# A triangular solve in an RWKV-7 layer: from 64x64 chunk matrices to compact 32x32 diagonal blocks

## The chip, the cores and the metric

The kernel runs on one core of one Trainium2 chip. The metric is the device time of one execution in microseconds (us). Times of one execution of the program lie within about 0.3% of each other, so a difference under that can't be told from none.

The engines are named as in the profile: PE is TensorE's matmul, PEld its weight load, DVE is VectorE, ACT is ScalarE, POOL is GpSimd, SP is SyncE, whose queue issues most transfers.

## The reference

Two decoder layers of width 1024 over 256 positions. Each layer mixes tokens with three branches (a gated linear recurrence, differential attention, RWKV-7), merges them with gates, and ends in a gated MLP. Only the RWKV-7 branch is touched. Per head (8 heads of 64), it computes

```python
def step(state, inp):
    r_t, w_t, k_t, v_t, a_t, b_t = inp
    sa = jnp.einsum("bhvk,bhk->bhv", state, a_t)
    state = (state * w_t[:, :, None, :] + sa[..., None] * b_t[:, :, None, :]
             + v_t[..., None] * k_t[:, :, None, :])
    return state, jnp.einsum("bhvk,bhk->bhv", state, r_t)
```

The kernel works in chunks of 64 positions. Within a chunk the recurrence over `sa` is a triangular system: with N the strictly lower triangular 64x64 matrix of the products of the a and b vectors of the chunk's positions (each scaled by its decays), the kernel needs T = (I - N)^-1 for every head and chunk: 8 heads x 4 chunks = 32 inverses a layer.

## The kernel before

Everything of the program is in `trunk_kernel`, with one block of code for each engine; the order of the work on each engine is written out by hand, and semaphores join them. For the merge of the branches TensorE has 576 matmuls a layer (12 token units of "gate" or "merge" weights, 128x128 weights with 512 columns moving; lines 1973, 1975 and 1979) which depend on nothing in the RWKV branch. A generator hands them out: `fill(point)` puts the next `FILL[point]` of them into TensorE's program at a point where it would otherwise wait for another engine, and what is left is issued after the branch.

The 32 matrices of a layer lie as `[128, 2, 8, 64]`: partitions 0 to 63 and 64 to 127 hold the first and the second chunk of a pair, then parity of the head (`par`), then 8 blocks (pair of chunks x head pair). One bank of PSUM holds the 8 blocks of one parity, 512 columns. In this layout the stages of the solve are, in the order of `STEPS`:

- "ak", "n", "nt" (TensorE, `chunk_products`, line 2075): the products of K and A, the matrix N, and N transposed, 32 products of 64x64 each, in four tiles of the array (2 row groups by 2 column groups). DVE reads them out with masks (lines 1499, 1501, 1491).
- The start: T of the 2x2 diagonal blocks is I + N restricted to them. ACT writes identities into T and its transpose TT (lines 874, 875), DVE adds the masked blocks of two (lines 1491, 1515).
- Then TensorE makes the products of AK with V (line 2098), which ACT reads (line 887).
- Five levels (`LEVELS`, block sizes 2, 4, 8, 16, 32), each with two steps for each parity: "m", the product of N and TT, read out by DVE with the level's mask (line 1519), and "x", the product of T with that, added to TT by DVE (line 1525). After every level but the last DVE transposes TT back into T by 32x32 blocks (line 1529); blocks of T beyond 32 aren't needed. A step of TensorE is 16 products of 64x64 (`block_products`, line 2084), on the two diagonal tiles of the array, 32 for both parities; a product in f32 stands in the trace as two weight loads and two matmuls.

After each step TensorE has 8 matmuls of `FILL` (6 after the last one). I call the two parities of a step with the fill behind them a slot; the five levels are ten slots a layer. Beside the reading, DVE takes other work in the solve by place in its program: `mod_beside(1)` (one weight block of the conditioning vectors, lines 1112 and 1115, which waits for a 512 KB transfer that POOL issues, line 560), `gated(2)` (line 1363), `dve_chunks` and `branch_low` (the low parts of weights and inputs, lines 1350 and 1400). POOL makes some low parts itself (line 586). SP's queue reloads the four slots of `ring` with 1 MB of weights each as TensorE finishes them (line 490); the masks are loaded once, in the first layer (lines 524 and 526).

```python
def block_products(b, a, bb, done):
    for m in range(8):
        for c in range(2):
            last = MM(ps[halves[c], b, m * 64:(m + 1) * 64], a[halves[c], m, :], bb[halves[c], m, :], start=True, stop=True)
            if m == 7:
                last.then_inc(done, 1)
```

## Time and profile before

| what | value |
|---|---|
| median of 3 runs | 1099.38 us (1097.0 to 1100.24) |
| the profiled execution | 1098.47 us, its span 1096.7 us |
| mean granted clock of TensorE | 0.992 of full |
| busy: PE, PEld, DVE, ACT, POOL | 1075.3, 989.9, 845.3, 582.7, 125.8 us |
| solve of layer 0 (first product to the last read-out) | from 209.5 to 261.1 us of the span |
| solve of layer 1 | from 745.2 to 793.3 us |

A row of the timeline gives start, duration, engine, line, operation, tile written and read, shape and count, and in brackets how long the engine was idle before it and what released it. "issue" as the releaser means that the engine waited for nothing that the profile shows.

### The profile page before, as it was taken

Reading aid. Unit: us, or ns where it says so; the run is one execution under the profiler, and the core shown is the slowest. Engines: PE = TensorE matmul, PEld = TensorE weight load, DVE = VectorE, ACT = ScalarE, POOL = GpSimd, SP = SyncE. Lnnn points to the kernel's source line nnn. Section 1 sums busy time; section 2 is a strip of 40 time slices with the busy share of each in tenths; the row PEclk is TensorE's granted clock in tenths of the full one; section 3 lists DMA queues with packets and bytes.
Section 4 is the critical chain, followed back from the end, with each engine's and each line's share of the span. In section 5 each row is a group of like instructions: output and inputs, shape, how many; then the busy total and the mean of one; then the engine's idle time right before and its main releaser. Section 6 shows DMA issues by size and latency. Waiting matters only on the chain.

```text
span 1096.7 us, 23323 instructions
## 1 busy us (share of the span) xinstructions
PE 1075.3 (98%) x9660; PEld 989.9 (90%) x9660; DVE 845.3 (77%) x1245; ACT 582.7 (53%) x894; POOL 125.8 (11%) x142
## 2 busy tenths in 40 slices
PE   8999999899999999999999999999999999999997
PEld 7889988787789999999989999878887999999997
DVE  4798998686578798987758899977755878888763
ACT  2266567532364666663355575683227466666533
POOL 0100000056002000001120000002640200000001
PEclk8999999999999999999999999999999999999999
DMA  9946455443156567667854546361615465555651
GB/s 378 342 172 217 178 172 225 180 154 139 42 208 235 188 233 245 218 234 292 311 189 167 206 157 223 144 229 60 232 59 192 154 244 184 186 191 191 222 201 39
DMA packets 41460, 214.81 MB, mean 196 GB/s; under 512 B 7936, under 2 KB 8320, under 8 KB 22048
## 3 DMA queue, kind: packets, MB, share of 16 engines
q1 hardware_dynamic: 29856, 171.65, 42.8%
q0 software_dynamic: 11520, 41.95, 10.8%
q8 instruction: 64, 1.05, 0.4%
q14 instruction: 20, 0.16, 0.0%
HBM read 212.01 MB, written 1.05 MB: 194 GB/s over the span
## 4 chain that ended last, share of the span: by engine, by line
PE 93%; DVE 4%; DMA 2%; issue 1%; ACT 1%; DVEq 0%; ACTq 0%
PE ps L1786 18%; PE ps L1784 17%; PE ps L1785 17%; PE ps L1975 6%; PE ps L1979 6%; PE ps L1973 6%; PE ps L1804 5%; PE ps L2084 2%; DMA mring<-wmod_dram 2%; PE ps L1743 1%; DVE macc L1115 1%; PE ps L2256 1%; PE ps L2075 1%; PE ps L1761 1%; PE ps L2000 1%
## 5 line engine op out<-in xcount | busy, mean ns | idle before, releaser
L965 ACT ACTIVATE WH<-ring 128x1024 fp32r<-128x1024 f32 x144 | 151.9, 1060 | 164.9 <-PE ps L1786 157.2
L1634 DVE TENSOR_TENSOR WLO<-ring,WH 128x1024 fp32r<-128x1024 f32 x144 | 175.8, 1234 | 70.0 <-ACT WH L965 70.0
L1786 PE MATMUL ps<-HH,WLO 128*128 128x256 f32 x736 | 208.1, 283 | 0.0
L1785 PE MATMUL ps<-HL,WH 128*128 128x256 f32 x736 | 206.6, 281 | 0.0
L1784 PE MATMUL ps<-HH,WH 128*128 128x256 f32 x736 | 205.0, 279 | 0.0
L1786 PEld LDWEIGHTS ps<-HH,WLO 128*128 128x128 f32 x736 | 138.7, 188 | 0.0
L1784 PEld LDWEIGHTS ps<-HH,WH 128*128 128x128 f32 x736 | 138.5, 188 | 0.0
L1785 PEld LDWEIGHTS ps<-HL,WH 128*128 128x128 f32 x736 | 138.0, 188 | 0.0
L560 POOL DMA_DIRECT2D mring<-wmod_dram x80 | 43.4, 542 | 763.2 <-DVE macc L1115 456.5
L1115 DVE SCALAR_TENSOR_TENSOR macc<-mring,sm,macc 128x1024 f32<-128x1024 f32 x70 | 96.5, 1378 | 16.4 <-DMA mring<-wmod_dram 14.4
L1786 PE MATMUL ps<-GH,WLO 128*128 128x256 f32 x384 | 108.3, 282 | 0.0
L1784 PE MATMUL ps<-GH,WH 128*128 128x256 f32 x384 | 108.2, 282 | 0.0
L1785 PE MATMUL ps<-GL,WH 128*128 128x256 f32 x384 | 107.9, 281 | 0.0
L1786 PE MATMUL ps<-HG,RLO 128*128 128x256 f32 x384 | 107.9, 281 | 0.0
L1662 DVE SCALAR_TENSOR_TENSOR TK<-ps,PR,TK 128x255 f32<-128x255 f32 x192 | 79.1, 475 | 0.0
L1979 PE MATMUL ps<-RLO,HG 128*128 128x512 f32 x192 | 77.7, 405 | 0.0
L1786 PEld LDWEIGHTS ps<-GH,WLO 128*128 128x128 f32 x384 | 73.7, 192 | 0.0
L1786 PEld LDWEIGHTS ps<-HG,RLO 128*128 128x128 f32 x384 | 72.5, 189 | 0.0
L1785 PEld LDWEIGHTS ps<-GL,WH 128*128 128x128 f32 x384 | 72.2, 188 | 0.0
L1784 PEld LDWEIGHTS ps<-GH,WH 128*128 128x128 f32 x384 | 72.1, 188 | 0.0
L778 ACT ACTIVATE WC<-ring 128x1024 fp32r<-128x1024 f32 x36 | 37.8, 1055 | 62.3 <-PE ps L1975 33.1
L1784 PE MATMUL ps<-HG,WCR 128*128 128x256 f32 x208 | 58.8, 283 | 0.0
(404 smaller groups left out, 2552.7 us busy)
## 6 DMA issues: line engine op xcount, KB each, us to landing
ring<-wmain_dram SPq DMA_DIRECT2D x150, 1024.0 KB, 4.9
mring<-wmod_dram POOLq DMA_DIRECT2D x80, 512.0 KB, 5.0
G<-wmod_dram SPq DMA_DIRECT2D x3, 1024.0 KB, 10.0
R<-wmod_dram SPq DMA_DIRECT2D x3, 1024.0 KB, 17.7
TK<-wmod_dram SPq DMA_DIRECT2D x2, 1024.0 KB, 20.5
X<-x_t_dram SPq DMA_DIRECT2D x1, 1024.0 KB, 5.8
y_dram<-H SPq DMA_DIRECT2D x4, 256.0 KB, 2.1
SW<-small_dram SPq DMA_DIRECT2D x1, 512.0 KB, 13.6
```

Source lines behind the costliest of these rows:

```text
L560: pool.dma_start(mring[:, n % 2, :], wmod[mod_row(n)]).then_inc(s_m[n % 2], 16)
L965: A(WH[:, n % 2, part], ring[:, b, part], ACT.Copy).then_inc(hi_ready, 1)
L1115: V.scalar_tensor_tensor(macc[:, u % 2, :], block, sm[:, CSIL + kt:CSIL + kt + 1], macc[:, u % 2, :], ALU.mult, ALU.add).then_inc(mod_used, 1)
L1634: V.tensor_tensor(WLO[:, n % 2, part], ring[:, b, part], WH[:, n % 2, part].bitcast(F32), ALU.subtract).then_inc(lo_ready, 1)
L1662: ins = V.scalar_tensor_tensor(UB[:, q % 2, t, d:S], duo(b)[:, t, 0:S - d], PR[:, l, bass.ds(j + (COL["fw"] + 48 * (2 - d)), 1)], UB[:, q ...
L1784: MM(out, w_high[:, at], high, start=start, stop=False, skip_group_check=True)
L1785: MM(out, w_high[:, at], low, start=False, stop=False, skip_group_check=True)
L1786: return MM(out, w_low[:, at], high, start=False, stop=stop, skip_group_check=True)
L1804: last = MM(ps[:, g % 4, m * S:(m + 1) * S], w_of(g, m, i), rhs[:, i, :], start=(i == 0), stop=(i == KT - 1))
L1973: MM(ps[:, b, :], high[:, tk], w_high, start=(k == 0), stop=False, skip_group_check=True)
L1975: i = MM(ps[:, b, :], low[:, tk], w_high, start=False, stop=False, skip_group_check=True)
L1979: i = MM(ps[:, b, :], high[:, tk], w_low, start=False, stop=(k == nk - 1), skip_group_check=True)
```

## The change

The matrices of the levels up to 16 become compact: only the two diagonal 32x32 blocks of each 64x64 matrix are kept, one on each quarter of 32 partitions, so that the matrices of one parity are `[128, 8, 32]`, and the four 32x32 tiles on the diagonal of the array work on them. Masks come in this shape too (`CN`, eight more DMAs in the first layer; `CM` keeps three masks).

- "n" is 64 products with 32x32 results (64 rows of weights, 32 columns; eight tiles); "nt" is gone, and "off" is new: 32 products for the block N[32:64, 0:32], which ACT copies to `No` (two copies of 128x256).
- The start: T = I + N masked, formed compactly (`Tn`), and its transpose `TTn` by DVE's 32x32 transposes in place of a product; ACT's two identities are gone.
- A step of a level below the last is 32 products of 32x32 per parity (64 for both) in place of 16 of 64x64; DVE reads 128x256 in place of 128x512.
- The last level is T22 N21 T11 alone: its "m" is 16 products per parity, its "x" 32, of which half multiply with an identity to bring the second diagonal block into place; DVE copies. Before it, one DVE operation ("left") writes the first diagonal block and zeros into the 64x64 `TTm`.
- `mod_beside(1)` of the "x" of the fourth level moves to the "m" of the last; the number is the same. `FILL` stays as it is.

```diff
-LEVELS = [M_U2, M_U4, M_U8, M_U16, M_U32]
+LEVELS = [N_U2, N_U4, N_U8, N_U16, None]
+LAST = len(LEVELS) - 1
...
+        Nn, No, Tn, TTn, Mn = [narrow_mats(a) for a in (4, 6, 8, 10, 12)]
...
+                    for g in range(4):
+                        rows = slice(Q * g, Q * g + Q)
+                        sp.dma_start(CN[rows, N_LOW:N_ID, :], consts[rows, AT_MASKS:AT_MASKS + N_ID * P]
+                                     .rearrange("p (n s) -> p n s", s=P)[:, :, Q * g:Q * g + Q]).then_inc(s_masks, 16)
+                        sp.dma_start(CN[rows, N_ID, :], consts[rows, Q * g:Q * g + Q]).then_inc(s_masks, 16)
...
-                A(TTm.rearrange("p g m s -> p (g m) s"), over(small_mask(M_ID), 16), ACT.Copy).then_inc(i_ready, 1)
-                A(Tm.rearrange("p g m s -> p (g m) s"), over(small_mask(M_ID), 16), ACT.Copy).then_inc(i_ready, 1)
...
+                for par in range(2):
+                    act.wait_ge(t_mm, SOLVED[-1] * l + products_until("off", par))
+                    A(No[:, par], narrow(4 + par), ACT.Copy).then_inc(off_ready, 1)
...
                     elif kind == "n":
-                        V.tensor_tensor(Nm[:, par], oct(b), over(small_mask(M_LOW), 8), ALU.mult).then_inc(t_ev, 1)
+                        V.tensor_tensor(Tn[:, par], narrow(b), over(narrow_mask(N_L1), 8), ALU.mult).then_inc(t_ev, 1)
+                        V.tensor_tensor(Nn[:, par], narrow(b), over(narrow_mask(N_LOW), 8), ALU.mult).then_inc(t_ev, 1)
                         if par:
                             for p2 in range(2):
+                                dve.wait_ge(t_ev, base + reads_until("begin", p2))
+                                V.tensor_tensor(Tn[:, p2], Tn[:, p2], over(narrow_mask(N_ID), 8), ALU.add).then_inc(step, tick(n_step))
                             for p2 in range(2):
+                                dve.wait_ge(step, n_step[0] - 1 + p2)
+                                V.transpose(flat(TTn[:, p2]), flat(Tn[:, p2])).then_inc(t_init, 1)
                             dve_chunks(18, 19)
...
+                    elif v < LAST:
+                        V.tensor_tensor(TTn[:, par], TTn[:, par], narrow(b), ALU.add).then_inc(t_ev, 1)
+                        if par == 1:
+                            for p2 in range(2):
+                                dve.wait_ge(t_ev, base + reads_until("x", p2, v))
+                                V.transpose(flat(Tn[:, p2]), flat(TTn[:, p2])).then_inc(t_turned, 1)
+                            if v == LAST - 1:
+                                V.tensor_scalar(TTm[:, :, :, 0:Q].rearrange("p g m s -> p (g m) s"), TTn.rearrange("p g m s -> p (g m) s"),
+                                                small_mask(M_U32)[:, CH - 1:CH], None, ALU.mult).then_inc(t_ev, 1)
+                                gated(2)
+                            else:
+                                mod_beside(1)
                     else:
-                        V.tensor_tensor(TTm[:, par], TTm[:, par], oct(b), ALU.add).then_inc(t_ev, 1)
...
+                        V.tensor_copy(TTm[:, par, :, Q:CH], narrow(b)).then_inc(t_ev, 1)
...
-                def block_products(b, a, bb, done):
+                def block_products(b, pairs_, done):
 
                     for m in range(8):
-                        for c in range(2):
-                            last = MM(ps[halves[c], b, m * 64:(m + 1) * 64], a[halves[c], m, :], bb[halves[c], m, :], start=True, stop=True)
+                        for g, a, bb in pairs_:
+                            last = MM(ps[quarters[g], b, m * Q:(m + 1) * Q], a[:, m, :], bb if len(bb.shape) == 2 else bb[:, m, :],
+                                      start=True, stop=True)
                             if m == 7:
                                 last.then_inc(done, 1)
...
-                chunk_products(6, KK, AB, t_mm)
-                pe.wait_ge(t_ev, base + 2)
-                chunk_products(4, AB, KK, t_mm)
+                narrow_products(6, [(g, g, g) for g in range(4)], t_mm)
+                pe.wait_ge(t_ev, base + reads_until("ak", 1))
+                narrow_products(4, [(1, 1, 0), (3, 3, 2)], t_mm)
```

## Rows read from the trace of the kernel before

**Rows 1.** The page: busy time by engine, and the queue that brings TensorE's code.

```profile
PE 1075.3 (98%) x9660; PEld 989.9 (90%) x9660; DVE 845.3 (77%) x1245; ACT 582.7 (53%) x894; POOL 125.8 (11%) x142
...
q8 instruction: 64, 1.05, 0.4%
```

**Rows 2.** Timeline of layer 1: the first two slots of the solve.

```profile
753.09 1.94 PEld L2084 LDWEIGHTS ps<-R 64*64 64x64 f32 x64 [0.36 <-issue]
...
754.86 1.28 DVE L1519 TENSOR_TENSOR R<-ps,CM 128x512 f32<-128x512 f32 x2
...
757.16 1.95 PEld L2084 LDWEIGHTS ps<-R 64*64 64x64 f32 x64 [0.36 <-issue]
...
759.92 1.30 DVE L1529 STREAM_TRANSPOSE R<-R 128x512 f32<-128x512 f32 x2
```

**Rows 3.** Windows of layer 0: slots, the opening, and two stretches with a gap.

```profile
core 0: us, PE busy (x) PEld busy (x) DVE busy (x) ACT busy (x) POOL busy (x), PEclk, DMA share, GB/s
...
209.50:212.30 2.80, 2.27 (x139) 2.13 (x140) 2.58 (x4) 0.00 (x0) 0.00 (x0) 1.00 0.60 237
212.30:214.60 2.30, 0.24 (x11) 0.11 (x5) 0.94 (x2) 0.00 (x0) 0.00 (x0) 0.98 0.08 29
214.60:218.00 3.40, 3.39 (x91) 3.39 (x92) 1.60 (x5) 0.00 (x0) 0.00 (x0) 0.51 0.02 5
221.00:225.10 4.10, 4.10 (x75) 3.40 (x74) 3.55 (x4) 2.59 (x4) 2.48 (x1) 1.00 0.02 4
...
237.30:241.40 4.10, 4.10 (x75) 3.41 (x74) 3.79 (x4) 4.00 (x8) 1.54 (x3) 1.00 0.81 299
...
258.30:261.90 3.60, 3.60 (x71) 2.98 (x71) 1.91 (x3) 0.00 (x0) 2.57 (x2) 1.00 0.43 146
265.50:271.00 5.50, 5.50 (x170) 4.38 (x168) 3.35 (x6) 1.29 (x3) 5.34 (x5) 1.00 0.52 194
```

**Rows 4.** Timeline of layer 1: 128-wide transposes, then 64x64 products in four and two tiles.

```profile
737.33 0.94 PEld L2062 LDWEIGHTS ps<-C,KK 128*128 128x128 f32 x8
...
745.22 1.02 PEld L2075 LDWEIGHTS ps<-KK,ZS 64*64 64x64 f32 x64 [0.35 <-issue]
...
749.04 1.94 PEld L2098 LDWEIGHTS ps<-TK,R 64*64 64x64 f32 x64 [0.17 <-DVE R L1501]
```

**Rows 5.** Timeline of layer 0: the two gaps of TensorE that no semaphore explains.

```profile
214.61 1.65 PE L2075 MATMUL ps<-KK,AB 64*64 64x64 f32 x51 [2.07 <-issue]
...
272.58 0.80 PE L2149 MATMUL ps<-R,TK 64*64 64x64 f32 x35 [1.40 <-issue]
```

**Rows 6.** DMA in windows 215.7:216.9, then 270.1:271.2 and 220:226 (40 slices each).

```profile
q8 instruction: 1, 0.02, 6.0%
...
DMA  0009000000000000000000000000000000000000
...
DMA  0000000400000000000000000000000000000000
```

**Rows 7.** Lines of the solve on DVE and ACT: one operation in ns (min, median, max).

```profile
L1491 DVE TENSOR_TENSOR E<-ps,CM x4: 415/420/425, 216.4 to 749.4; 128x256 f32<-128x256 f32 x4
...
L1529 DVE STREAM_TRANSPOSE R<-R x16: 662/685/706, 227.8 to 786.8; 128x512 f32<-128x512 f32 x16
...
L874 ACT ACTIVATE R<-CM x2: 1042/1043/1044, 198.2 to 734.0; 128x1024 f32<-128x1024 f32 x2
```

**Rows 8.** Timeline of layer 0: ACT before its reading, and one of DVE's conditioning blocks.

```profile
218.10 0.60 ACT L887 ACTIVATE WY<-ps 128x512 f32<-128x512 f32 x1 [8.82 <-PE ps L2098]
...
247.21 1.28 DVE L1115 SCALAR_TENSOR_TENSOR macc<-mring,sm,macc 128x1024 f32<-128x1024 f32 x1 [1.80 <-DMA mring<-wmod_dram]
```

**Rows 9.** Timeline of SP's queue: the masks and the next weights.

```profile
34.62 4.26 SPq L524 DMA_DIRECT2D CM<-consts_dram  x1
...
41.84 3.37 SPq L526 DMA_DIRECT2D CM<-consts_dram  x1
46.90 67.29 SPq L490 DMA_DIRECT2D ring<-wmain_dram  x12
```

More of the change, by code:

```diff
@@ L185, with tiles_used, solve_reads, products_until @@
 STEPS = solve_steps()
-NSTEP = len(STEPS)
-SOLVED = [int(n) for n in np.cumsum([1 if k in ("ak", "n", "nt") else 2 for k, _, _, _ in STEPS])]
-def step_no(kind, par, v):
-    return next(i for i, s in enumerate(STEPS) if s[:3] == (kind, par, v))
+def tiles_used(kind, v):
+    return {"ak": 1, "n": 4, "off": 2, "m": 2 if v == LAST else 4, "x": 4}[kind]
+SOLVED = [int(n) for n in np.cumsum([tiles_used(k, v) for k, _, v, _ in STEPS])]
+def solve_reads():
+    reads = []
+    for kind, par, v, _ in STEPS:
+        if kind == "n":
+            reads += [("begin", par, 0), ("n", par, 0)]
+        elif kind != "off":
+            reads.append((kind, par, v))
+        if (kind, par, v) == ("x", 1, LAST - 1):
+            reads.append(("left", 0, 0))
+    return reads
+READS = solve_reads()
+NREAD = len(READS)
+def products_until(kind, par, v=0):
+    return SOLVED[next(i for i, s in enumerate(STEPS) if s[:3] == (kind, par, v))]
+def reads_until(kind, par, v=0):
+    return READS.index((kind, par, v)) + 1
 def trunk_kernel(nc, wmain, wmod, small, v1v2, params, consts, lqk, x_t, positions, y_t):
@@ L370, in oct, with narrow @@
             return ps[:, b, :].rearrange("p (m s) -> p m s", s=CH)
+        def narrow(b):
+            return ps[:, b, 0:8 * Q].rearrange("p (m s) -> p m s", s=Q)
         def by_chunk(ap, c):
@@ L1487, in _ @@
                 dve_chunks(17, 18)
-                def blocks_of_two(at, src, mask, odd):
-                    m = over(every_other(small_mask(mask), odd), 8)
-                    return V.tensor_tensor(E[:, at, :].rearrange("p (j n) -> p j n", j=8), every_other(src, odd), m, ALU.mult)
-                dve.wait_ge(s_masks, 64)
-                base = NSTEP * l
+                dve.wait_ge(s_masks, 192)
+                base = NREAD * l
                 mm0 = SOLVED[-1] * l
                 for n, (kind, par, v, b) in enumerate(STEPS):
+                    if kind == "off":
+                        continue
                     dve.wait_ge(t_mm, mm0 + SOLVED[n])
@@ L2064, in _ @@
                 fill(7)
-                base = NSTEP * l
+                base = NREAD * l
                 halves = [slice(64 * i, 64 * i + 64) for i in range(2)]
+                quarters = [slice(Q * i, Q * i + Q) for i in range(4)]
                 def chunk_products(b0, a, bb, done):
```

83 lines of the change are left out of this document (43 added, 40 removed).

## The prediction, made before the changed kernel was run

> **What bounds the kernel now.** I read the page first: PE is busy for 98% of the span [rows 1], so what counts in any stretch is TensorE's own stream, unless the change makes it wait. Then the timeline of the solve. A slot of layer 1 starts at 753.09 and the next at 757.16, a period of 4.07 us [rows 2]: 64 pairs of weight load and matmul (32 products, two pairs each) and 8 matmuls of the fill behind them. DVE reads out and transposes beside this, two operations in 1.28 and 1.30 us [rows 2], and isn't what the slot ends on: in the windows of 221.0 and 237.3 PE is busy throughout [rows 3]. ACT idles 8.82 us before its reading [rows 8]. So the solve is bound by TensorE.
>
> Then the rate of TensorE. In two tiles 64 pairs begin within 1.94 us [rows 2]; less one load's 0.135 this is 28.7 ns a pair, or 57 ns a pair on each tile. In four tiles 64 pairs take 1.02 us [rows 4], 14 ns a pair, again 56 ns on each tile. So the tile sets the pace and not the issue, at least down to 14 ns. Eight 128-wide pairs take 0.94 us [rows 4], 107 ns each: width costs about 0.8 ns a column, with some 5 ns beside it.
>
> Last the gaps that no semaphore explains. In layer 0 TensorE stops twice in the middle of a run of small products, until 214.61 and until 272.58, and the profile says "issue" [rows 5]. The queue named instruction brought 64 packets and 1.05 MB [rows 1], 16 KB each. One of them begins in the fourth of 40 slices of the window from 270.1, at 270.2, and takes some 0.97 us; PE resumes 1.4 us after it has landed [rows 5, 6]. Counting instructions back from the gap at 212.3, 279 began since 209.5 [rows 3]; counting back from the second, the 338 of the window from 265.5 [rows 3] put the 256th before the stop at about 267.0. I read this as: a packet is 256 instructions (128 pairs), two packets fit, and the next is asked for when the last begins to run. From that moment until the new one runs it was 209.7 to 214.6, 4.9 us, and 267.0 to 272.6, 5.6 us. The transfers were busy then (0.60 and 0.52 of the DMA engines [rows 3]). With nothing else to carry, the packet of the window from 220 begins at 221.1 [rows 6], at once, and would have run 1.0 + 1.4 = 2.4 us after the request; the one in the window from 215.7 had been asked for at 214.6, so 3.7 us. Now a slot spends 72 pairs in 4.07 us, 128 pairs in 7.2, and this costs nothing. It is the part of the machine that the change leans on.
>
> **What the change does to TensorE, part by part.** A layer's "n" and "nt" are 128 pairs now, at 14 ns: 1.8 us. The ten steps are 640 pairs at 28.7 ns: 18.4 us. After, "n" and "off" are 192 pairs, the steps 8 x 128 + 64 + 128 = 1216 pairs, 32 columns wide. No row shows such a pair. By the tile's pace of 0.8 ns a column and 5 ns it takes 30 ns on its tile, in four tiles 7.6 ns. If each pair still took 14 ns, the least seen, the steps would come to 17.0 us and the slot would stay as it is. I take 7.6, because two tiles and four gave the same pace per tile, and keep 14. The slot would then be 4.07 - 1.84 + 0.97 = 3.2 us. Unbound by anything else this gives 18.4 - 9.2 = 9.2 us a layer in the steps and 0.4 us in the opening, 19 us in all.
>
> The Trainium skill ("TensorE: Matmul & The Clock Gate", section "Wait — 56ns, not 53.3ns?") says that the start of a matmul never follows that of the last within about 25 ns, however narrow. By that the slot would be 4.07 - 1.84 + 3.2 = 5.4 us, and the change a loss of some 25 us. The trace doesn't agree: its 64 pairs in 1.02 us are 14 ns apart.
>
> But the code has to come. After, a slot is 136 pairs and some waits, 1.07 packets. Four slots lie where the DMA engines are nearly idle (0.02 at 221.0), six where they are busy (0.81 at 237.3, 0.43 at 258.3) [rows 3].
> - The four quiet slots: 4.3 packets, each the larger of 3.0 us (its run time at 3.2 us a slot) and 2.4 to 3.7 us for the fetch, say 3.15: 13.5 us for 16.3 now. -2.8 us.
> - The six busy ones, of which one has 64 pairs less: 5.9 packets at 2.4 to 5.6 us, of which those under 3.0 count as 3.0; I take 4.2, a bit over the middle, since the busy transfers are packed closer. 24.8 us, where now it is 237.3 to 261.9, 24.6 us [rows 3]. +0.2 us.
> - The opening has 320 pairs in place of 256, and less time in them. In layer 0 the packet awaited at 212.3 still comes at 214.6. What follows in it, 128 pairs, is through in 1.3 us where it took until 221.0 less the fill, and the next packet runs at 214.6 + 3.7 = 218.3. The rest of AK by V at 30 ns (1.6 us) and the fill (some 2.4 us) end at 222.3, for 221.0 now. +1.2 us, in layer 1 taken the same.
>
> The sum is -1.4 us a layer. Beside it the clock: after the 2.3 us gap of layer 0 its granted share was 0.51 from 214.6 to 218.0 [rows 3], a loss of 1.7 us. Layer 1 has no such gap now and gets one; at even chances +0.9 us, 0 to 1.7. And DVE's conditioning blocks: one already waited 1.80 us for its transfer [rows 8], and it is asked for relatively later; +0.4 us (0 to 3). In all -2.8 + 1.3 = -1.5 us on the executed 1098.47, which lies 0.9 us under the median.
>
> **What costs nothing, and what hides it.** DVE reads 256 columns at 0.42 us for 0.68, and transposes in about the same ratio from 0.685 [rows 7]: 28 operations a layer save about 7 us, which keeps pace with TensorE's shorter slot; without it DVE would have bound, since it is busy 3.5 to 4.0 of each 4.1 us now [rows 3]. The new operation "left" (0.4 to 0.7 us) stands in the slot that loses a conditioning block of 1.3 us. ACT loses two copies of 1.04 us [rows 7] outside the path and gets two of 0.4 us before its reading of AK by V, inside an idle time of 8.82 us [rows 8]; without that cover, 0.8 us. SP issues 12 mask transfers for 4: those took from 34.6 to 45.2, and the next weights followed at 46.9 [rows 9], so 1.7 us are free, and I guess 2 to 6 us more. The weights land 5 us after the issue and aren't used before 59; if that cover were gone, it would cost up to 4 us once. POOL's queue is passed by nothing.
>
> **The rivals.**
> (1) The code keeps up (0.24). The fetch was seen to bind twice, both times with busy transfers, and could start earlier when the request is not behind a wait. Then the 3.2 us slot holds: -9.2 - 0.4 a layer, given back 2 us a layer to conditioning blocks that come late: about -15 us, 1084 us. The Trainium skill ("Runtime: NRT & Kernel Launch", section "Instruction fetch mechanics") has it so: crossing a block of 256 instructions is mostly hidden. The two gaps speak against this as a rule.
> (2) The issue floor lies near 14 ns (0.12). Then TensorE saves nothing in the slots, the packets come nearly in time, and the result is 0 to +4 us: 1101 us.
> (3) The other side (0.14): gaps beget a slow clock. The place is the busy half of the solve, where a packet may come 2.5 us late; the price is the 1.7 us that the stretch from 214.6 shows. If such a gap comes in three of the six slots of each layer, this is +5 a layer, with the gaps' own time in the sum above at 5.6 us a packet (5.9 x 5.6 = 33.0, +8.4 a layer) about +23 us, 1122 at the most, 1110 in the middle. It decides once the gaps reach about 2 us. For it: DMA at 0.81 and more for whole slots. Against: the slots have 1.9 us of full-width fill each, and the second gap of layer 0 left the clock alone.
> That the change doesn't compute in 32x32 tiles side by side (each product waiting for the last one: 30 ns a pair) I count within (3): two tiles do overlap within one bank [rows 2].
>
> **The numbers.** The forecast has 0.50. Less than 0.3% (3.3 us) can't be told from no change here. Its own range is 8 us less to 6 us more: of its 0.50, 0.14 are faster, 0.27 the same, 0.09 slower. (1) adds 0.22 faster and 0.02 same; (2) 0.07 same and 0.05 slower; (3) 0.14 slower. So faster 0.36, same 0.36, slower 0.28. Time: 1098.47 + 0.9 - 1.5 = 1097.9, say 1098. The likeliest case's own range is 1091 to 1105. The range for 8 in 10 reaches into (1) and (3): 1087 to 1110.
>
> **What would show it.** In the changed trace: runs of 128 pairs in about 1.0 us where they aren't interrupted (7.6 ns a pair), or 1.8 (rival 2). Slots of 3.2 to 3.5 us in the quiet stretch and of 4 to 5 in the busy one, with PE's idle time put down to "issue", and packets of the instruction queue 3 to 5 us apart, each 1.4 us ahead of the resumption. Ten more packets on the page, 74 for 64 (1280 more instructions a layer are five). A gap near 747.3 in layer 1. I am wrong if the slots are 3.2 us throughout, if PE waits for DVE and not for "issue", or if the granted clock falls under 0.98.

## The result and the profile after

The changed kernel took 1119.85 us (median of 4 runs, 1113.06 to 1124.19), the kernel before beside it 1098.19 us: a ratio of 1.019, 95% interval 1.0142 to 1.0239. It is slower by some 21 us (1.9%), where 1098 us were forecast and 1110 us closed the range. The four runs of the changed kernel lie 1.0% apart, more than the 0.3% given ahead for one program; the intervals take that in. The profiled execution is the fastest of the four: 1113.06 us, span 1111.2 us, mean granted clock 0.982 (0.992 before).

The page of the changed kernel, sections 1, 3 and 4:

```profile
PE 1072.7 (97%) x10940; PEld 983.6 (89%) x10940; DVE 827.5 (74%) x1243; ACT 580.2 (52%) x894; POOL 125.1 (11%) x142
...
q8 instruction: 74, 1.21, 0.4%
...
PE 93%; DVE 3%; issue 3%; ACT 1%; POOL 1%; DMA 0%; DVEq 0%; ACTq 0%
```

The busy time of PE hardly fell (1075.3 us before), although half of the time of the levels' products was to go, 18 of 37 us over both layers; the queue named instruction has its 74 packets, for 64 [rows 1]; and "issue" has 3% of the chain, 33 us, where the page of the kernel before has 1%. What PE waited for, by line and releaser:

```profile
PE ps L2135 <- issue: 14.4, 8, 4.0
...
PE ps L2126 <- issue: 3.7, 2, 2.1
PE ps L2017 <- issue: 1.3, 1, 1.3
```

Each row gives the total in us, how often, and the longest. L2135 is the products of the levels, L2126 those of "n" and "off". The kernel before had the two gaps of [rows 5]. The view has no row in which L2135 waits for DVE. In the timeline of PE, one undisturbed slot, a gap in a quiet stretch, and the worst one:

```profile
224.87 1.56 PE L2135 MATMUL ps<-R 32*32 32x32 f32 x128
226.36 0.50 PE L2011 MATMUL ps<-WCG,HG 128*128 128x512 f32 x1
...
764.56 0.49 PE L2013 MATMUL ps<-WCG,HGL 128*128 128x512 f32 x1 [0.20 <-issue]
764.98 1.37 PE L2135 MATMUL ps<-R 32*32 32x32 f32 x127
768.57 0.21 PE L2135 MATMUL ps<-R 32*32 32x32 f32 x1 [2.21 <-issue]
...
775.39 1.65 PE L2135 MATMUL ps<-R 32*32 32x32 f32 x128
...
779.00 1.14 PE L2135 MATMUL ps<-R 32*32 32x32 f32 x99
784.12 0.64 PE L2135 MATMUL ps<-R 32*32 32x32 f32 x29 [3.99 <-issue]
```

The fill starts 1.49 us after the first of 128 pairs (226.36 for 224.87). In the slot of the kernel before, 64 pairs start at 753.10 in the timeline of PE and the first matmul of the fill at 755.11, 2.01 us later. The starts of 128 pairs that nothing disturbs span 1.20 us, 9.4 ns a pair, for 1.86, and such slots follow each other in 3.37 us (221.50 to 224.87), for 4.07: some 0.7 us shorter. But then a slot stops in its middle for 3.99 us. The transfers while it waits:

```profile
q1 hardware_dynamic: 42, 0.34, 67.6%
q0 software_dynamic: 39, 0.15, 32.2%
q8 instruction: 1, 0.02, 4.9%
```

This is the window from 781.5 to 782.7. Queues 1 and 0 (the weight ring and the conditioning blocks) fill the DMA engines, and the one packet of code among them lands at 782.62, 1.5 us before PE resumes. All the larger gaps look so: 1.4 to 1.6 us lie between a landing and the resumption at 246.04 and 247.44, 767.0 and 768.57, 802.85 and 804.39. Counting back 256 instructions from each resumption, as the prediction did, gives the request: from request to run it is 3.4 to 4.0 us for packets in the quiet stretches (222.1 to 225.55, 232.6 to 236.17, 764.56 to 768.57), and 5.2, 6.1 and about 7.6 us for those that ran at 241.31, 247.44 and 784.12.

The gap that ends at 768.57 has the DMA engines almost to itself (nothing but the packet of code from 765.5 until 767.0), and still lasts 2.21 us. What sets it apart is what its packet holds: the one that began at 764.56 is one matmul of the fill and 127 narrow pairs, some 1.8 us of work against 4.0 us until the next one runs. A packet with eight matmuls of the fill in it lasts 3.2 us and hides most of the fetch. So it is the work of each packet that counts, and not the mean of a slot.

The ten slots of layer 0 in the kernel before, from the first product to the end of the last, with columns as in [rows 3]:

```profile
221.00:260.40 39.40, 38.80 (x714) 32.34 (x713) 33.60 (x38) 11.22 (x15) 22.73 (x15) 1.00 0.47 172
```

Those of the changed kernel, layer 0 and layer 1, then some of its stretches at half the clock:

```profile
221.50:262.00 40.50, 34.76 (x1292) 27.61 (x1292) 28.65 (x40) 10.55 (x14) 22.04 (x15) 0.96 0.46 163
757.80:805.00 47.20, 36.94 (x1290) 28.82 (x1290) 24.09 (x40) 11.26 (x15) 22.90 (x15) 0.88 0.42 148
...
565.10:568.50 3.40, 3.40 (x10) 2.69 (x9) 3.30 (x6) 3.37 (x8) 0.57 (x1) 0.50 0.00 0
...
769.90:773.30 3.40, 3.40 (x133) 2.52 (x131) 0.95 (x2) 0.00 (x0) 2.55 (x2) 0.50 0.34 99
783.60:790.40 6.80, 6.28 (x166) 4.92 (x165) 2.69 (x5) 1.06 (x1) 3.77 (x3) 0.50 0.42 144
804.00:807.40 3.40, 3.01 (x10) 1.84 (x9) 0.42 (x1) 0.00 (x0) 0.00 (x0) 0.50 0.02 5
...
sum 34.00, PE 31.73 PEld 26.16 DVE 16.44 ACT 9.82 POOL 9.82; mean PE 3.97 PEld 3.27 DVE 2.05 ACT 1.23 POOL 1.23
```

Layer 0 is no shorter than before and layer 1 is 7 to 8 us longer. Leaving out the start and the end of the program, TensorE has 34.0 us at 1.2 GHz in eight stretches, where the kernel before has two of 3.4 us. Five of the eight, 23.8 us, come with the five gaps of 2 us and more: that at 783.6 begins 0.5 us before its gap of 3.99 us ends, that at 804.0 0.4 us before the end of one of 3.31 us, that at 769.9 1.3 us behind one of 2.21 us. The other three (565.1, 739.2 and 896.2) have no gap over 0.45 us near them, and lie outside the solves. If time at half the clock costs half of itself, which is an estimate (the fill ran at half its pace there, the narrow pairs at 13.4 ns for 9.4), 27.2 us more of it is 13.6 us: 10.2 with the gaps, 3.4 without.

The balance of the two profiled executions: by the spacing of their pairs, the products of the slots give back 2 x 6.8 us = 13.6 us. Idle time of PE in gaps over 0.45 us rose from 6.7 to 22.6 us, +15.9, and the clock took 13.6. That makes +15.9; the spans differ by 14.5, since some idle time falls into the stretches at half clock and so is counted twice. By place: +1.0 us up to the state chain of layer 0 (its start of the solve was 1.5 us earlier, the solve 2.5 us longer), +2.3 between the solves, +9.9 in the solve of layer 1 (63.3 us to the reading products, for 53.4) and +1.2 behind it. The 3.5 us between and behind the solves, where nothing was changed, are about the size of the falls of the clock there, so they need not be an effect of the change.

### The profile page after: what moved, and what is told of

Its sections match the earlier page's. It is cut to its first block, busy times and chain, and to the rows that moved or that the text cites. A ratio compares the mean times of both kernels' runs of the same rounds, so it can differ in the third digit from the quotient of the medians.

```text
span 1111.2 us, 25891 instructions
## 1 busy us (share of the span) xinstructions
PE 1072.7 (97%) x10940; PEld 983.6 (89%) x10940; DVE 827.5 (74%) x1243; ACT 580.2 (52%) x894; POOL 125.1 (11%) x142
## 4 chain that ended last, share of the span: by engine, by line
PE 93%; DVE 3%; issue 3%; ACT 1%; POOL 1%; DMA 0%; DVEq 0%; ACTq 0%
PE ps L1824 17%; PE ps L1822 17%; PE ps L1823 17%; PE ps L2013 6%; PE ps L2017 6%; PE ps L2011 6%; PE ps L1842 5%; PE ps L2135 3%; PE ps L1781 1%; PE ps L2314 1%; PE ps L1799 1%; PE ps L2038 1%; PE ps L1968 1%; DVE RLO L1623 1%; PE ps L2100 1%
## 5 line engine op out<-in xcount | busy, mean ns | idle before, releaser
L1154 DVE SCALAR_TENSOR_TENSOR macc<-mring,sm,macc 128x1024 f32<-128x1024 f32 x70 | 92.1, 1316 | 15.7 <-DMA mring<-wmod_dram 13.2
L817 ACT ACTIVATE WC<-ring 128x1024 fp32r<-128x1024 f32 x36 | 37.8, 1055 | 69.8 <-PE ps L2013 43.9
L1842 PE MATMUL ps<-H,ring 128*128 128x256 f32 x256 | 60.2, 397 | 0.9 <-DVE H L1186 0.5
## 6 DMA issues: line engine op xcount, KB each, us to landing
SW<-small_dram SPq DMA_DIRECT2D x1, 512.0 KB, 14.4
```

What stands on the lines that cost most here:

```text
L1154: V.scalar_tensor_tensor(macc[:, u % 2, :], block, sm[:, CSIL + kt:CSIL + kt + 1], macc[:, u % 2, :], ALU.mult, ALU.add).then_inc(mod_used, 1)
L1842: last = MM(ps[:, g % 4, m * S:(m + 1) * S], w_of(g, m, i), rhs[:, i, :], start=(i == 0), stop=(i == KT - 1))
```

## The experiments

Ratios are to the kernel before, run beside it on the same chip, with 95% intervals; a time without an interval is one run, read for its trace and not for its time. "The after" is the changed kernel.

### Is it the code? Fewer products, more fill, pairs by themselves

**More fill between the products.** Edit of the after: 10 matmuls of fill instead of 8 (6 at the last) at each of eleven points, and `gated(2)` moved a slot forward with them.

```diff
-FILL = [8, 32, 48, 32, 36, 8, 20, 8] + [8] + [8, 8] * 4 + [8, 6]
+FILL = [8, 32, 48, 32, 36, 8, 20, 8] + [10] + [10, 10] * 4 + [10, 10]
```

> The changed kernel with 10 matmuls of the fill behind each step of the solve in place of 8 (11 points, the total of the kernel unchanged), and one DVE read of a merge bank a slot earlier so that they can run. Theory A (the code of TensorE comes too slowly: a packet of 128 weight-load and matmul pairs needs 3.4 us at least and up to 6 us under load): a packet then lasts 0.4 us longer per slot, so the stalls called issue shrink by 5 to 8 us over both layers and one to three of the slow-clock stretches go; the time falls by 4 to 12 us against the changed kernel's 1120 us. Rival B (32-wide products are slow in themselves, by issue or by tile): the work is only moved, the time stays within 2 us.

1142.96 us, 1.0409 (1.0367 to 1.0451): a miss. The gaps in the products stayed (14.0 us put down to "issue" at L2135, for 14.4), although a slot had two matmuls more. They still end 1.3 to 1.6 us behind a landing, but this run doesn't bear out that a little more work in each packet shortens them; why it doesn't stays open. And the fill, pulled forward, came to its weights' low parts too soon (6.8 us of waiting for L1389). It shows what a pause can cost, though. The windows before and after such a wait:

```profile
285.00:289.70 4.70, 3.03 (x80) 2.77 (x80) 2.34 (x4) 0.00 (x0) 4.70 (x5) 1.00 0.00 0
289.70:323.80 34.10, 33.43 (x169) 26.24 (x170) 8.91 (x11) 1.99 (x5) 2.34 (x2) 0.50 0.20 77
```

A wait of 2.34 us (288.03 to 290.37), and the clock stayed at half for 34.1 us, though PE was busy through 33.4 of them. The record of the clock is no artefact: matmuls of the fill began every 0.43 us there, for 0.23 at the full clock.

**Twice the pairs at half the width**, to price a pair. Edit of the before: each 64x64 product in two of 32 moving columns.

```diff
-    last = MM(ps[halves[c], b, m * 64:(m + 1) * 64], a[halves[c], m, :], bb[halves[c], m, :], start=True, stop=True)
+    for s in (0, 32):
+        last = MM(ps[halves[c], b, m * 64 + s:m * 64 + s + 32], a[halves[c], m, :], bb[halves[c], m, s:s + 32], start=True, stop=True)
```

> The kernel before, with each 64x64 product of the ten steps issued as two products of 32 moving columns: the same result, 128 pairs in each slot as in the changed kernel, but no other part of the change. Theory A: undisturbed a slot's products take 2.4 us or less in place of 1.86, the slot 4.6 us or less, a packet 4.3 us, so the quiet slots gain no stall and the busy ones do: 5 to 15 us slower than before, with resumptions 1.4 us after a code packet has landed, and 5 more packets a layer. Rival B: slower by the products' own time alone, 10 x 0.5 us a layer, 10 us, with no stall that no semaphore explains. The two are told apart by the gaps, not by the total.

1133.87 us, 1.0332 (1.0291 to 1.0374), 37 us more where 5 to 15 were expected. The pairs of a slot:

```profile
224.21 3.94 PE L2085 MATMUL ps<-R 64*64 64x32 f32 x128
```

Their starts span 3.72 us, 29.3 ns a pair in two tiles: what a pair with 64 moving columns takes. So the 57 ns that I had read as the price of 64 moving columns is the price of the 64x64 weights. The period of a slot became 5.93 us and no product of the slots waited for code, with as many pairs in a slot as the after has: the time per packet matters, not the count.

**The pairs alone**, at the end of the before: 512 products with 32x32 weights in the four diagonal tiles, then 512 with 64x64 weights and 32 columns.

```diff
+            for n in range(512):
+                g = n % 4
+                q4 = slice(32 * g, 32 * g + 32)
+                MM(ps[q4, 5, n // 4 % 16 * 32:n // 4 % 16 * 32 + 32], ones[q4, 0:32], ones[q4, 0:32], start=True, stop=True)
...
```

> The kernel before with a run of 512 products of 32x32x32 in the four diagonal tiles at TensorE's end (1024 pairs, 8 packets of code, nothing else to transfer), then 512 products of 64x64 weights by 32 moving columns in two tiles (1024 pairs). Theory A: bursts of 128 pairs in 1.2 us (9.4 ns a pair), then a wait until 1.4 us after the next packet has landed, a period of about 3.4 us for 128 pairs, 27 us for each of the two runs. Rival B: an even rate without gaps, 9.4 ns a pair or whatever the tile allows: 10 us for the first run. The second run also gives the pace of a 64x64 weight load with 32 columns: by the tile 18 ns a pair.

1171.1 us. The timeline of PE:

```profile
1088.93 1.28 PE L2324 MATMUL ps<-ones 32*32 32x32 f32 x128 [2.19 <-issue]
1093.23 1.93 PE L2324 MATMUL ps<-ones 32*32 32x32 f32 x128 [3.02 <-issue]
1096.70 1.93 PE L2324 MATMUL ps<-ones 32*32 32x32 f32 x128 [1.54 <-issue]
1100.72 1.93 PE L2324 MATMUL ps<-ones 32*32 32x32 f32 x128 [2.09 <-issue]
...
1104.46 1.93 PE L2324 MATMUL ps<-ones 32*32 32x32 f32 x128 [1.81 <-issue]
```

and two windows of it:

```profile
1100.00:1114.00 14.00, 7.84 (x494) 7.37 (x495) 0.00 (x0) 0.00 (x0) 0.00 (x0) 0.50 0.02 5
1120.00:1140.00 20.00, 20.00 (x380) 20.00 (x380) 0.00 (x0) 0.00 (x0) 0.00 (x0) 0.50 0.01 2
```

This is the clearest row of the study. Bursts are of exactly 128 pairs, 256 instructions. The second follows the first in 4.30 us, with the output's transfer beside it; from there on they follow each other every 3.47 to 4.02 us, 3.75 at the end, with no other transfer (DMA share 0.02). So code comes at 128 pairs in about 3.75 us when it is asked for like this, and PE ran them in 1.09 (8.5 ns a pair, in the one burst shown at full clock). And the clock was at half: from 1090.5, in the first pauses, through the second set of products, in which PE was busy all the time. There a pair with 64x64 weights took 53 ns, for 29.3 at the full clock.

The Trainium skill has this otherwise ("Runtime: NRT & Kernel Launch", section "Instruction fetch mechanics"): the next block of 256 instructions is fetched while one executes, and the crossing is "mostly hidden". That holds here as long as a packet's work takes longer than the 3.4 to 4.0 us of a quiet fetch, as in the slots of the before; it fails for narrow products.

**Half of the products left out** of the ten slots of the after (blocks 4 to 7 of the inverses are not computed in its levels, and DVE adds half as much in the "x" steps).

```diff
-                    for m in range(8):
+                    for m in range(4):
                         for g, a, bb in pairs_:
...
```

> The changed kernel without half of the products of the ten steps (the second four of the eight blocks; their inverses stay at the start's value, and DVE adds half as much in the x steps): 64 pairs in a slot again, 32 wide. Theory A (packets of code of 128 pairs, at least 3.4 us apart): a slot is 0.6 + 0.37 + 1.86 = 2.85 us, a packet 5 us; the gaps called issue in the slots vanish but for one or two of the busiest, and with them the slow-clock stretches there; ten slots in 29 to 32 us in both layers (changed kernel: 40 and 47). Rival B (narrow products are slow to switch or to issue): half of the gaps stay and ten slots take 34 us or more.

1107.53 us. Quiet slots came to 2.82 us and every code gap in the slots was gone, but the ten slots still took 37.8 and 37.5 us, a miss. PE's waits name the next bound (L2136 is the products of the levels here, L2127 those of the opening):

```profile
PE ps L2136 <- DVE R L1558: 11.3, 6, 4.6
PE ps L2127 <- issue: 4.9, 2, 2.9
```

### What lies under the code: VectorE's conditioning blocks

**The blocks moved away**, all eight of a layer behind the state chain (their transfers too), in the after.

```diff
                         elif par == 1:
-                            mod_beside(1)
...
+                mod_beside(8)
                 dve.wait_ge(gg_ready, 4 * (l + 1))
```

> The changed kernel with the seven conditioning blocks of each layer's solve (their transfers by POOL and their DVE work) put behind the state chain; the total will be longer, since they are then waited for, and is not what is looked at. Theory A: with fewer transfers beside it a code packet is carried sooner; in the solve no slot loses more than 2.5 us, and the ten slots of a layer take 33 to 38 us in place of 40 (layer 0) and 47 (layer 1). Rival C (DVE's conditioning blocks, waiting for their transfers, hold the steps): also shorter, but the gaps called issue stay as they were. If the slots stay at 40 and 47 with the same gaps, the lag of the packets has another source.

1148.38 us. The slots took 38.9 us in layer 0 and 42.2 in layer 1, a miss (33 to 38 were expected), and kept 10.9 us of code gaps, with 5.9 us more in the opening; and TensorE waited 29.8 us behind the state chain, where the moved blocks stand before low parts of weights. Against the kernel before (39.4 us), taking away either bound alone gains 2 us a layer at the most and loses 3 in one; against the changed kernel it does help in layer 1 (47.2 us). Taking away both:

> The changed kernel with half of the products of its ten steps left out (64 instructions of a slot's 128 pairs, its numbers wrong for it) and, also, its eight conditioning blocks of the solve and state chain moved behind the state chain: both suspected bounds off at once. Theory (two bounds lie stacked, code delivery and VectorE's blocks, each of which alone keeps the ten slots at 37 to 40 us): here the slots follow TensorE's own work, about 2.8 to 3.0 us each, so ten slots take 28 to 31 us from the first slot's start to the end of the last, and the idle of TensorE within them is under 2 us a layer. Rival (a third bound: VectorE's reads, masks and transposes of the steps themselves, or ScalarE and the loads of fill weights): ten slots stay over 34 us though no conditioning block and no code gap stands in them. The whole time tells little, since the moved blocks are waited for later (29.8 us in the run that moved them alone): 1105 to 1145 us.

1115.4 us with the same two edits together (the same products left out). The ten slots as windows:

```profile
222.80:249.00 26.20, 26.20 (x682) 20.14 (x682) 15.98 (x32) 10.66 (x15) 18.23 (x8) 1.00 0.33 123
763.00:791.30 28.30, 26.44 (x682) 20.20 (x682) 14.55 (x32) 11.25 (x15) 18.77 (x8) 1.00 0.32 114
```

The slots ran at 2.81 us in both layers, 26.2 and 28.3 us for ten (one code gap of 1.85 us in layer 1), where each edit alone left 38 to 42. Two bounds lie one on the other about the slot of the before, at 3.7 to 4.2 us on average.

**Fast products with half the code**: the before, with both parities of a step together in the four 64x64 tiles, the odd parity crossing from one half of the partitions to the other and back.

```diff
+    for m in range(8):
+        for par in range(2):
+            for c in range(2):
+                fr, to = (c, c) if par == 0 else (c, 1 - c) if kind == "m" else (1 - c, c)
+                last = MM(ps[halves[to], b + par, m * 64:(m + 1) * 64], a[halves[fr], par, m, :], bb[halves[fr], par, m, :], ...)
```

> The kernel before with both parities of a step issued together in all four 64x64 tiles: the odd parity's m product is written to the other half of the partitions, T of that parity is kept there (DVE's transposes in two halves), and its x product comes back. The number of products and of instructions is that of before, 64 pairs a slot, in 1.0 us in place of 1.86 by the pace of four tiles. Theory A: 72 pairs in 3.2 us or more are a packet in 5.7 us, which code delivery allows outside the busiest transfers; DVE has 7.0 us of work in two slots and becomes the bound: 3.5 us a slot, 5 to 14 us faster than before. Rival B (any shortening of the products is lost): within 3 us of before.

1107.0 us, 1.012 (1.0063 to 1.0178), a miss. A slot's products take 0.94 us and quiet slots 3.15 to 3.25, with no code gap among them. DVE is what is late now:

```profile
PE ps L2093 <- DVE R L1530: 11.7, 6, 4.2
PE ps L2093 <- DVE R L1524: 11.2, 7, 2.6
```

and its own timeline, with POOL's beside it, tells why:

```profile
230.81 2.38 POOL L586 TENSOR_TENSOR RLO<-ring,WC 128x1024 fp32r<-128x1024 f32 x1
...
231.03 3.25 DVE L1115 SCALAR_TENSOR_TENSOR macc<-mring,sm,macc 128x1024 f32<-128x1024 f32 x1
234.20 1.27 DVE L1530 TENSOR_TENSOR R<-R,ps 128x512 f32<-128x512 f32 x2
...
243.25 1.28 DVE L1115 SCALAR_TENSOR_TENSOR macc<-mring,sm,macc 128x1024 f32<-128x1024 f32 x1 [3.70 <-DMA mring<-wmod_dram]
```

A block takes 1.28 us alone and 3.25 here beside POOL's operation, and it may wait 3.70 us for its transfer, with the read-out of the products queued behind it. Both were there before ([rows 8] shows a wait of 1.80 us), inside a slot that was long enough. The Trainium skill ("SBUF — State Buffer", section "Who interferes with whom") calls the port pair that VectorE and GpSimd share an exclusive lock; the rows agree, 3.25 us being about the block's 1.28 behind most of POOL's 2.38.

With the blocks moved behind the state chain, as above:

> The kernel before with both parities of a step in four 64x64 array tiles (slot products 0.94 us instead of 1.86) and the eight conditioning blocks of a layer moved behind the state chain. Theory (the four-tile version lost because VectorE, behind its conditioning blocks and their transfers, could not follow a shorter slot): the waits of the slots for VectorE's reads, 23 us in the run with the blocks in place, fall under 5 us, quiet and busy slots alike take 3.1 to 3.3 us, ten slots of a layer 31 to 33 us. The blocks are then waited for later, so the whole time is not lower for it: 1105 to 1150 us. Rival (the four-tile form itself slows VectorE, by its partition-crossing transposes and longer dependence from product to product): the waits for VectorE's reads stay over 12 us.

1111.03 us, 1.0116 (1.008 to 1.0153). The waits of the slots for DVE fell from 22.9 to 2.0 us and ten slots took 30.9 us; the waits came back as 27.8 us behind the state chain, as expected.

### The parts of the change that help, and where the blocks belong

**Only the first twin by vector transposes**, in the before: "nt" is left out, and DVE transposes T once it is formed.

```diff
-    steps = [("ak", 0, 0, 4), ("ak", 1, 0, 5), ("n", 0, 0, 6), ("n", 1, 0, 7), ("nt", 0, 0, 4), ("nt", 1, 0, 5)]
+    steps = [("ak", 0, 0, 4), ("ak", 1, 0, 5), ("n", 0, 0, 6), ("n", 1, 0, 7)]
...
+                            for p2 in range(2):
+                                dve.wait_ge(step, n_step[0] - 1 + p2)
+                                V.transpose(flat(TTm[:, p2]), flat(Tm[:, p2])).then_inc(t_init, 1)
```

> The kernel before with one part of the change alone: the product for N transposed is gone, T of the start is formed as before and its twin by DVE's 32x32 transposes. TensorE loses 64 pairs and one wait for DVE a layer (0.9 + 0.7 us) and half a packet of code, DVE keeps its 2.8 us. Theory A: 2 to 5 us faster than before, no new gap. If it is slower, DVE's start is on the path.

1094.9 us, 0.9979 (0.9965 to 0.9994): this part of the change gains some 2.3 us (0.7 to 3.8). Together with the four 64x64 tiles:

> The two edits of e6 and e7 together. Theory A: their gains add, 7 to 17 us faster than before, 1080 to 1090 us. If code delivery takes it back: less than the better of the two alone, with gaps called issue in the busy slots.

1104.52 us, 1.0077 (1.0057 to 1.0097), a miss: the two gains don't add, and PE waits 21.8 us for DVE's reads. And the twin with the last level on its one off-diagonal block, in the wide layout:

> The kernel before with the first transposed twin by vector transposes (the version that ran at 0.998 of before) and, also, the last level on its one off-diagonal 32x32 block, in the wide layout: the same number of instructions, but with 32x32 weights, 16 pairs to a parity in two array tiles. Theory (in this form the slots are bound by the loading of 64-column weights, some 29 ns a pair, and the code comes in time): the two slots of the last level have products of about 0.5 to 1.0 us instead of 1.86, which saves 0.9 to 1.4 us in each, 2 to 5 us in all with two layers; some comes back as a wait for VectorE, which then has to copy two blocks of 32 partitions. Total 1091 to 1096 us, ratio to before 0.993 to 0.998. Rival (all that a shorter slot gives up is taken by code or VectorE at once, as in the changed kernel): 1096 to 1100 us.

1096.4 us, 0.9977 (0.9957 to 0.9997): no more that can be told than the twin alone. A slot of the last level in it:

```profile
249.18 1.29 PE L2095 MATMUL ps<-R 32*32 32x32 f32 x64
250.40 0.51 PE L1981 MATMUL ps<-RLO,YH 128*128 128x512 f32 x1
```

The fill starts 1.22 us after the first product, for 2.01, and PE waits 1.42 us for DVE's read-out in each layer instead. The starts of the 64 pairs span 1.10 us, 17.4 ns a pair in two tiles, or 35 ns on a tile with 32x32 weights, where 64x64 weights with the same 32 moving columns took 58.6. Whether the rows or the columns of the weights make the difference isn't separated.

**The blocks where VectorE waits.** Edit of the version with twin and four 64x64 tiles: of eight blocks a layer three stay in the slots, one stands before the state chain and four in it, where DVE waited 1.2 to 3.8 us for TensorE with all eight moved away. Their transfers move too, so that POOL's chunks no longer stand behind a wait for DVE.

```diff
-                    if i < 7:
-                        mod_blocks(m1 + i, m1 + i + 1)
+                    if i in (2, 4, 6):
+                        mod_blocks(m1 + i // 2 - 1, m1 + i // 2)
...
+                mod_blocks(m1 + 3, m1 + 4)
...
                                 gated(2)
-                            mod_beside(1)
...
                 gated(3)
+                mod_beside(1)
...
-                        if c == 1:
-                            mod_beside(1)
+                        mod_beside(1)
+                mod_beside(1)
```

> The kernel before with the first transposed twin by vector transposes and both parities of a step in four 64x64 array tiles (together 1.0077 of before), and now the eight conditioning blocks of a layer spread over the places where VectorE waits: one in each of three slots, one behind the reads before the state chain, four in the state chain, where the trace of the version with all eight moved shows VectorE waiting 1.2 to 3.8 us for TensorE at each step; GpSimd's transfers of the blocks move with them, so its chunk work no longer waits for VectorE. Theory (the four-tile slots lost only because the blocks stood in them, and the blocks cost nothing where VectorE waits): the ten slots of a layer take 31.5 to 34 us instead of 40, TensorE waits less than 3 us a layer for VectorE's reads and less than 3 us for low parts of weights, and each layer is 4 to 9 us shorter than in the kernel before. Total 1080 to 1092 us, ratio to before 0.983 to 0.995. Rival (the time that the solve gives up is taken back behind it, by fill work that has been used up or by transfers that come late, as a wait of TensorE between the state chain and the next stage): 1094 to 1108 us.

1077.35 us, 0.9822 (0.9783 to 0.9862). It beats both kernels, by 20 and by 42 us. The windows of its ten slots, PE's waits on them, and DVE in the state chain:

```profile
216.00:247.30 31.30, 29.72 (x713) 23.12 (x713) 28.33 (x39) 11.00 (x15) 21.90 (x11) 1.00 0.43 154
738.40:769.70 31.30, 29.70 (x713) 23.07 (x713) 28.32 (x39) 11.04 (x15) 21.87 (x11) 1.00 0.40 149
```

```profile
PE ps L2092 <- DVE R L1523: 2.9, 6, 0.8
```

```profile
268.27 1.22 DVE L1350 TENSOR_TENSOR RLO<-ring,WC 128x1024 fp32r<-128x1024 f32 x1
269.41 1.28 DVE L1115 SCALAR_TENSOR_TENSOR macc<-mring,sm,macc 128x1024 f32<-128x1024 f32 x1
```

Ten slots take 31.3 us in each layer, the clock is at 1.00, DVE is busy for 28.3 of them, and the block at 269.41 fills what was a wait of 1.29 us in the run with all eight moved. The last two runs separate the placement from the form of the products. The same placement in the after:

> The changed kernel with its eight conditioning blocks a layer spread as in the version at 0.982 of before (three in the slots, one before the state chain, four in it). Theory (code delivery is a bound of its own, 128 pairs in no less than 3.4 us and up to 6 us under ring loads, and falls of the clock follow its gaps): TensorE still idles 6 to 14 us over both solves in gaps that end 1.3 to 1.5 us after a packet has landed, ten slots of a layer take 35 to 38.5 us, and the kernel comes to 1088 to 1112 us: better than the changed kernel (1120), but 10 us or more behind the version in four 64x64 tiles (1077) whose slots need half the code. Rival (the blocks' transfers were what held the packets up, and the blocks what held the slots): slots of 3.1 to 3.4 us throughout, 1070 to 1085 us.

1112.23 us, 1.0148 (1.0101 to 1.0194): 35 us behind. PE's waits, the gap in a slot of layer 0, and the ten slots of each layer:

```profile
PE ps L2135 <- issue: 12.3, 8, 3.0
PE ps L2126 <- issue: 5.8, 2, 4.3
```

```profile
243.29 0.38 PE L2135 MATMUL ps<-R 32*32 32x32 f32 x21
246.71 1.70 PE L2135 MATMUL ps<-R 32*32 32x32 f32 x107 [3.04 <-issue]
```

```profile
224.00:262.80 38.80, 33.73 (x1167) 26.26 (x1169) 19.83 (x34) 11.48 (x15) 19.66 (x10) 0.91 0.36 125
759.50:796.00 36.50, 31.22 (x1161) 24.59 (x1160) 19.13 (x34) 11.06 (x15) 19.29 (x10) 1.00 0.38 132
```

DVE is idle for half of these slots (busy 19.8 us of 38.8), and the code still comes late. And the same placement in the kernel before, its products as they were:

> The kernel before, with nothing changed but where its eight conditioning blocks of a layer stand (three in the slots, one before the state chain, four in it). Theory (its slots of 4.1 us are bound by TensorE's own work and hide the blocks; a block hinders only a shorter slot): the slots stay at 4.07 to 4.1 us, only those above that (the last three of a layer) lose their excess, 0 to 2 us a layer; total 1092 to 1098 us, ratio 0.995 to 1.001. Rival (the placement itself is most of the gain of the version at 0.982): 1080 to 1088 us.

1096.24 us, 0.9988 (0.9966 to 1.001): nothing. So neither the placement nor a faster product gains by itself, and the two together with the twin gain 20 us, 18 more than the twin alone, as long as the code of a slot stays at 64 pairs.

## Why the prediction was wrong

- **The mechanism was named, and it is the one that decides; the steps that failed are the prices of a packet of code and of the clock.** Runs of 128 pairs, packets of 256 instructions, waits put down to "issue" that end about 1.4 us after a landing, 74 packets, a gap near 747.3 (at 751.7): all there. With DVE's conditioning blocks spread, the changed kernel still has 18.1 us of waits for "issue", as many as without, and with half of the products left out it has none in its slots.
- **"2.4 to 3.7 us for the fetch, say 3.15" failed.** I took 2.4 from a packet whose transfer began "at once" with the request that I counted. Code was not short there. In the kernel before the same count has two more begin within 0.2 us of the request (226.81, 234.54) and one 1.1 us ahead of it (248.51), so where code isn't short the count doesn't give the moment of the request. In the changed trace none of those traced back began sooner than 0.9 us after it, and a quiet one takes 3.4 to 4.0 us from request to run; in the run of the pairs alone the packets come 3.47 to 4.02 us apart. So the quiet slots, too, are bound by code: four of them took 14.2 us in layer 0 and 17.6 in layer 1 (757.78 to 775.39), for 13.5. The 17.6 have a second cause, the mean over a slot: the packet of 764.56, with almost no fill in it, left a gap of 2.21 us.
- **"7.6 ns a pair" failed by a quarter.** It is 9.4 in the kernel, 8.5 alone. The working took a tile's pace to go by the width of the product; the split products show that the moving columns don't set it, the size of the weights does. Worth 1.8 x 127 ns = 0.23 us a slot, some 4 us in all; the undisturbed slot is 3.37 us, for 3.2. The Trainium skill's floor of 25 ns from start to start ("TensorE: Matmul & The Clock Gate", section "Wait — 56ns, not 53.3ns?") is further off still: the traces have 8.5 and 9.4 ns.
- **"2.4 to 5.6 us, I take 4.2" for a busy packet was too low.** The three traced back above took 5.2, 6.1 and 7.6 us, two of them outside the bounds, whose upper end came from two packets only. Ten slots up to the next stage's first product were forecast at 13.5 + 24.8 = 38.3 us, for 40.9 before, and took 41.4 in layer 0 (221.50 to 262.93) and 49.6 in layer 1 (757.78 to 807.38), half clock included. The opening took 2.0 us more than before in layer 0 and 1.3 in layer 1, for 1.2 forecast.
- **"+0.9 us for the clock" is the largest miss: 13.6 us in the profiled execution, 10.2 of it with gaps.** I priced one fall, of 1.7 us, in the opening of layer 1. Five stretches came with gaps, for one in the kernel before, and three without, for one. The prediction's rival (3) had this mechanism, with 0.14, 1110 us as its middle and 1122 at the most. Its condition (a gap of about 2 us in three of the six busy slots of each layer) was met in size but not in place: 2.12 and 2.60 us in layer 0, the first of them in the opening, and 2.21, 3.99 and 3.31 in layer 1, the first in the quiet slots. What I set against it, that the second gap of layer 0 left the clock alone, was one gap of 1.4 us and told nothing of those over 2 us. Over the traces of all the kernels here but the one with the pairs alone, start and end left out, 37 of the 43 gaps of 2 us or more come with a stretch at half the clock that begins in them or within 2 us behind them, and 3 of the 53 between 1 and 2 us; 21 stretches of 3.4 us come without any such gap. With about 2 us of a gap seen to cost 1.7 us more in the kernel before, the losing side had deserved more than its 0.28.
- **The wait for DVE's blocks (+0.4) did not come**: the code came later still. It was the second bound, hidden behind the first, as the 11.3 us of the run with half of the products show.
- The gain of the first twin, which the sum had not set apart, is real, 2.3 us.

How much of the +21 us is idle time and how much is the clock can't be read to the microsecond: runs of the after lie between 1113 and 1124 us, and only the fastest has a trace. The clock has most of the spread, though: its mean was 0.982 and 0.981 in the runs of 1113 and 1116 us and 0.973 and 0.975 in those of 1124, which by the estimate above is 7 to 10 of the 8 to 11 us. What makes the clock fall at one gap and not at another stays open as well, as does how the requests queue behind the other transfers: those of the busy packets began 2.8 to 5.0 us after their request, for 0.9 to 1.6 in the quiet.

## What to carry to other kernels

Small products have a price in code: before cutting matmuls into more and narrower ones, divide the instructions of the stretch by 256 and hold the time of each packet, not the mean, against 3.4 to 4.0 us, and 5 to 7.6 us where weights are being loaded. If the faster form has fewer instructions (four 64x64 tiles: 64 pairs in 0.94 us), take that one. Then ask what stands next, here VectorE's side work in a slot that was just long enough for it, and move it to where that engine waits: with either step alone the kernel was no faster, with both and the twin it gained 1.8%. And count a pause of TensorE of 2 us or more as longer than it is: in the changed kernel each of the five brought 3.4 or 6.8 us at half the clock.

## What the runs showed of the hardware

- A pair (weight load and matmul) with 64x64 f32 weights takes 57 to 60 ns on its tile, with 64 moving columns as with 32; four tiles side by side begin a pair every 15 ns (64 in 0.94 us). With 32x32 weights it is 17.4 ns in two tiles and 8.5 to 9.4 in four.
- TensorE's code arrives in packets of 16 KB, 128 pairs, 3.47 to 4.02 us apart with the DMA engines otherwise idle, and where TensorE waits for a packet, its work starts 1.2 to 1.6 us after the transfer has ended.
- The granted clock can stay at 0.50 while PE is busy without a pause: for 34.1 us with a wait of 2.34 us at its start, and for a whole set of products with 64x64 weights behind the bursts. Of 43 gaps of 2 us or more, 37 came with a stretch at 0.50.
- DVE's 128x1024 operation with two inputs from SBUF takes 1.28 us alone and 3.25 us beside POOL's of 2.38 us.
